# A transformer block on one Trainium2 core: retention on dense query columns, slot tables by one product, final scaling four tiles behind

## What is computed

```python
proj = h @ w_in                      # 4688 columns, two parallel head groups
y_a = dsa_attention(qa, ka, va, qi, ki, wi)    # indexer scores, top-256 keys, 8 heads
y_b = retention(qb, kb, vb, gb)                # 8 heads of 64
x = x + gt1 * (concat(y_a, y_b) @ w_o)
x = x + gt2 * hier_moe(h2)           # 2 of 32 SwiGLU experts for each token
return rmsnorm(x, g_final)
# retention, for each head, by chunks with a running state:
scores = (q @ k.T) * decay;  inner = scores @ v
cross  = (q @ state) * xi;   state = state * g_chunk + (k * zeta).T @ v
y = group_norm(inner + cross) * silu(g)
```

## Time and profile before

| | us |
|---|---|
| median of 3 runs | 1657.19 (1653.68 to 1657.38) |
| the profiled execution | 1657.88 |
| its span, first to last instruction | 1655.4 |
| PE busy | 1476.1 (89%) |
| DVE busy | 1124.7 (68%) |
| ACT busy | 913.5 (55%) |
| POOL busy | 267.4 (16%) |

### The profile page before, as it was taken

How to read it: one execution, slowest core, us unless ns; L and a number is a source line. 1 busy time by engine, 2 the same in 40 slices (tenths; PEclk the granted TensorE clock), 3 DMA queues, 4 the chain that set the end, 5 groups by cost and what they waited for, 6 DMA issues and landing times.

```text
span 1655.4 us, 21644 instructions
## 1 busy us (share of the span) xinstructions
PE 1476.1 (89%) x7444; PEld 1155.5 (70%) x7444; DVE 1124.7 (68%) x1511; ACT 913.5 (55%) x1231; POOL 267.4 (16%) x192
## 2 busy tenths in 40 slices
PE   3899999999999898888899967999999999999950
PEld 2587455888887787455666646888888888888840
DVE  6632798662256983434444365999999999999937
ACT  5321577879994111424444414777777777777722
POOL 0000110330001011200000001322322332332114
PEclk9899999999999999589999976999999999999985
DMA  9198543222324234211221017999999999999966
GB/s 369 61 340 317 207 153 115 96 108 97 121 71 134 71 121 148 91 51 65 80 66 45 22 51 273 378 402 401 403 400 400 393 401 398 397 394 398 362 239 256
DMA packets 102566, 368.01 MB, mean 222 GB/s; under 512 B 11232, under 2 KB 23648, under 8 KB 77792
## 3 DMA queue, kind: packets, MB, share of 16 engines
q1 hardware_dynamic: 74208, 291.58, 46.2%
q10 hardware_dynamic: 17024, 41.95, 6.6%
q0 software_dynamic: 11264, 33.57, 5.6%
HBM read 306.24 MB, written 69.21 MB: 227 GB/s over the span
## 4 chain that ended last, share of the span: by engine, by line
PE 76%; DVE 13%; ACT 4%; issue 3%; DMA 2%; POOL 2%; SPq 0%; DVEq 0%; ACTq 0%; POOLq 0%
PE PS L1638 19%; PE PS L1640 19%; PE PS L1639 19%; PE PS L1739 3%; PE PS L1762 2%; PE PS L1960 2%; PE PS L1848 2%; PE PS L1835 1%; DMA WK<-in_w_ada 1%; DVE wlo L1553 1%; DVE WK L1045 1%; PE PS L1695 1%; POOL BIG L730 1%; PE PS L1935 1%; DVE ACC L1158 1%
## 5 line engine op out<-in xcount | busy, mean ns | idle before, releaser
L1553 DVE TENSOR_TENSOR wlo<-raw,whi 128x2048 fp32r<-128x2048 f32 x192 | 435.8, 2285 | 36.4 <-ACT whi L956 34.9
L956 ACT ACTIVATE whi<-raw 128x2048 fp32r<-128x2048 f32 x192 | 364.0, 1913 | 130.1 <-DVE WK L1572 80.8
L1638 PE MATMUL PS<-whi,xhi 128*128 128x512 f32 x512 | 203.7, 398 | 7.3 <-DVE xlo L1559 6.1
L1640 PE MATMUL PS<-whi,xlo 128*128 128x512 f32 x512 | 201.1, 393 | 0.0
L1639 PE MATMUL PS<-wlo,xhi 128*128 128x512 f32 x512 | 200.1, 391 | 0.0
L837 ACT ACTIVATE KV<-ACC,WK 128x1024 int8<-128x1024 f32 (+4 forms) x160 | 147.5, 926 | 23.7 <-DVE WK L1181 21.1
L1638 PE MATMUL PS<-KVR,BIGR 128*128 128x512 f32 x320 | 127.0, 397 | 1.1 <-ACT WK L822 1.1
L694 POOL COPY wcol<-tw 128x1 f32 (+1 forms) x32 | 64.3, 2009 | 381.7 <-DVE WK L1590 377.3
L1640 PE MATMUL PS<-KVR,BIGR 128*128 128x512 f32 x320 | 124.9, 390 | 0.0
L1639 PE MATMUL PS<-KVR,BIGR 128*128 128x512 f32 x320 | 124.5, 389 | 0.0
L1638 PEld LDWEIGHTS PS<-whi,xhi 128*128 128x128 f32 x512 | 97.0, 190 | 27.6 <-DVE xlo L1559 7.0
(11 more groups left out here) (331 smaller groups left out, 2960.4 us busy)
## 6 DMA issues: line engine op xcount, KB each, us to landing
raw<-in_w_gate SPq DMA_DIRECT2D x64, 1024.0 KB, 7.3
raw<-in_w_up SPq DMA_DIRECT2D x64, 1024.0 KB, 7.8
raw<-in_w_down SPq DMA_DIRECT2D x64, 1024.0 KB, 7.2
y_dram<-zero ACTq DMA_DIRECT2D x8, 3072.0 KB, 11.3
WK<-in_w_ada POOLq DMA_DIRECT2D x16, 1024.0 KB, 7.5
y_dram<-WK ACTq DMA_DIRECT2D x32, 512.0 KB, 7.0
KV<-in_w_in SPq DMA_DIRECT2D x5, 2048.0 KB, 10.0
KV<-in_x SPq DMA_DIRECT2D x16, 512.0 KB, 5.2
```

The source lines that it names most:

```text
L956: nc.scalar.activation(whi[:, slot], raw[:, q], ACT.Copy).then_inc(G("m_hi"), 1)
L1553: V.tensor_tensor(wlo[:, slot], raw[:, q], whi[:, slot].bitcast(F32), ALU.subtract)\
L1638: mm(out_, x_hi, w_hi, start=first, stop=False)
L1640: return mm(out_, x_lo, w_hi, start=False, stop=final)
```

## The change

Four things, told by what they do.

Retention. The turned queries are kept dense (`qT`, 512 columns) and not block-diagonal. Scores are eight products of 64 rows and 128 columns, one for a head, the even heads on rows 0 to 63 and the odd ones on rows 64 to 127, in different banks. The constant `carry` that scales the state after each tile is zero outside the two diagonal blocks, so that one product of 128 columns gives the state's part for two heads. ACT makes one copy of 128 rows instead of two of 64. POOL's memset of `qBD` goes.

Slot tables. `tbl` and `tw` come from one product of 100 columns for each group of copies, where there were two of 50. DVE therefore multiplies by the weights (`sw`) before it signals each half. `items` without the number of rounds is written first of all, SP reads the number of rounds only after the three written-out slots, and DVE splits the first gate half of slot 0 before it copies the tables.

Final stage. DVE scales tile t - 4 after it has added tile t, with cells of its own for each tile's sum, mean and root.

```diff
-    parts["carry"] = np.tile(np.repeat(np.exp(P * lg), HD)[None], (P, 1))
+    parts["carry"] = np.where(p[:, None] // HD == np.arange(HB * HD)[None] // HD % 2,
+                              np.repeat(np.exp(P * lg), HD)[None], 0.0)
...
+            rounds = rounds()
             with engine.Fori(0, rounds) as j:
...
-            rounds = nc.sync.value_load(items[0:1, 63:64], min_val=1, max_val=MOST_ROUNDS)
...
+            def load_rounds():
+                sp.wait_ge(G("r_items"), 2)
+                return nc.sync.value_load(items[0:1, 63:64], min_val=1, max_val=MOST_ROUNDS)
...
-            for j in range(4):
-                pool.wait_ge(G(f"st_ev{j}"), 16 * 8)
-            own(nc.gpsimd.memset(WB["qBD"].rearrange("p j h n -> p (j h n)"), 0.0), G("b_clear"))
...
-                    act.wait_ge(G("b_clear"), 1)
-                pq = PS[:, 4, :].rearrange("p (j n) -> p j n", j=4)
-                own.go(A(WB["qBD"][0:64, :, 0, :], pq[0:64], ACT.Copy))
-                own.go(A(WB["qBD"][64:128, :, 1, :], pq[64:128], ACT.Copy), G("b_qbd"))
+                    for j in range(4):
+                        act.wait_ge(G(f"st_ev{j}"), 16 * 8)
+                own.go(A(WB["qT"], PS[:, 4, :].rearrange("p (j n) -> p j n", j=4), ACT.Copy), G("b_qbd"))
...
-                    own.go(V.tensor_tensor(WB["S"][:, 4 * half:4 * half + 4],
+                    own.go(V.tensor_tensor(WB["S"].rearrange("p (j a) n -> p a j n", a=2)[:, half],
...
+            dve.wait_ge(G("r_pe"), 3)
+            own(V.tensor_copy(items[0:1, 0:MAX_ITEMS], PS[0:1, 3, 0:MAX_ITEMS]), G("r_items"))
             for e, name in enumerate(("e1", "e2")):
                 own(V.tensor_tensor(WR["tmp"], WR[name], WR["V"], ALU.mult))
...
-                                       r16[:, some].unsqueeze(2).to_broadcast([P, 8, P]), ALU.is_equal), G("r_oh"))
-            own.wait()
-            for e in range(2):
-                some = slice(8 * e, 8 * e + 8)
+                                       r16[:, some].unsqueeze(2).to_broadcast([P, 8, P]), ALU.is_equal))
+                own.wait()
                 own.go(V.tensor_tensor(ohi[:, some, 1], ohi[:, some, 1],
                                        sw[:, e, :].unsqueeze(2).to_broadcast([P, T, TBL]), ALU.mult), G("r_oh"))
...
+            low(0, 0, GATE[0])
             dve.wait_ge(G("r_acc"), 1)
             own(V.tensor_scalar(tbl[:, :], PS[:, 2, 0:TBL], float(NO_TOKEN), None, ALU.add), G("r_done"))
-            dve.wait_ge(G("r_acc"), 2)
-            own(V.tensor_copy(tw[:, :], PS[:, 4, 0:TBL]), G("r_done"))
+            own(V.tensor_copy(tw[:, :], PS[:, 2, TBL:2 * TBL]), G("r_done"))
...
-                if t >= 2:
-                    f_finish(t - 2)
+                if t >= LAG:
+                    f_finish(t - LAG)
...
-                for j in range(4):
-                    last = mm(PS[:, 6 + j // 2, 256 * (j % 2):256 * (j % 2) + 256], WB["kT"][:, j, :],
-                              WB["qBD"][:, j].rearrange("p h n -> p (h n)"), start=True, stop=True)
+                for h in range(HB):
+                    rows = slice(HD * (h % 2), HD * (h % 2) + HD)
+                    last = mm(PS[:, 6 + h % 2, P * (h // 2):P * (h // 2) + P], WB["kT"][rows, h // 2, :],
+                              WB["qT"][rows, h // 2, :], start=True, stop=True)
...
-                    o = PS[:, 4, HD * h:HD * h + HD]
-                    if t >= 1:
-                        mm(o, WB["qBD"][:, h // 2, h % 2, :], WB["st"][:, h // 2, HD * (h % 2):HD * (h % 2) + HD],
+                    if t >= 1 and h % 2 == 0:
+                        mm(PS[:, 4, HD * h:HD * h + 2 * HD], WB["qT"][:, h // 2, :], WB["st"][:, h // 2, :],
                            start=True, stop=False)
-                    last = mm(o, WB["S"][:, h, :], WB["v"][:, HD * h:HD * h + HD], start=(t == 0), stop=True)
+                    last = mm(PS[:, 4, HD * h:HD * h + HD], WB["S"][:, h, :], WB["v"][:, HD * h:HD * h + HD],
+                              start=(t == 0), stop=(t == 0 or h % 2 == 1))
...
-            for a, bank in ((0, 2), (1, 4)):
-                for n in range(2 * T):
-                    if n % T == 0:
-                        pe.wait_ge(G("r_oh"), 2 * a + n // T + 1)
-                    last = mm(PS[:, bank, 0:TBL], WR["ohp"][:, n], WR["ohi"][:, n, a], start=(n == 0), stop=(n == 2 * T - 1))
-                last.then_inc(G("r_acc"), 1)
+            for n in range(2 * T):
+                if n % T == 0:
+                    pe.wait_ge(G("r_oh"), n // T + 1)
+                last = mm(PS[:, 2, 0:2 * TBL], WR["ohp"][:, n], WR["ohi"][:, n].rearrange("p a n -> p (a n)"),
+                          start=(n == 0), stop=(n == 2 * T - 1))
+            last.then_inc(G("r_acc"), 1)
```

More of the change, by code:

```diff
@@ L38 @@
 SPLIT_AT = 4
+LAG = 4
 STEP_SPEND = 5.0
@@ L300, in block_kernel @@
         items = sb("items", [1, 64], I32)
-        f_ms = [small[:, 55 + s:56 + s] for s in range(2)]
-        f_rs = [small[:, 57 + s:58 + s] for s in range(2)]
+        f_sq, f_ms, f_rs = [[small[:, T * n + t:T * n + t + 1] for t in range(T)] for n in range(3)]
         PS = ctx.enter_context(nc.psum_tensor("PS", [P, 8, 512], F32))
@@ L452, in steps @@
             step(2 * rounds + PEELED, 1, True)
+            return rounds
         def count(rounds):
@@ L725, in f_root @@
                 pool.wait_ge(G("norm_ms"), 2 * T + t + 2)
-                own(tt(f_rs[t % 2], f_ms[t % 2], expo[:, 0:1], ALU.pow), G("norm_rs"))
+                own(tt(f_rs[t], f_ms[t], expo[:, 0:1], ALU.pow), G("norm_rs"))
             for t in range(T):
@@ L1006, in _ @@
                 act.wait_ge(G("f_sum"), t + 1)
-                own(A(WF["sq"], WF["x"][t], ACT.Square, accum_out=small[:, 53 + t % 2:54 + t % 2]), G("norm_sq"))
+                own(A(WF["sq"], WF["x"][t], ACT.Square, accum_out=f_sq[t]), G("norm_sq"))
         @block.vector
@@ L1480, in _, with low @@
                     own(V.tensor_copy(L[:, TILES[i], :], PS[:, 7, 0:36]), G("b7_free"))
+            def low(i, s, q):
+                n, slot = place(i, s, q)
+                dve.wait_ge(G("m_hi"), n + 1)
+                V.tensor_tensor(wlo[:, slot], raw[:, q], whi[:, slot].bitcast(F32), ALU.subtract)\
+                    .then_inc(G("m_lo"), 1)
             spend(1000.0, last_choice)
@@ L1505, in _ @@
                 own(V.tensor_reduce(WR["row"][:, e], WR["tmp"], X_AXIS, ALU.add))
-            own(V.tensor_scalar(WR["h"][0:1, 0:MAX_ITEMS // 2], c("even")[0:1, :], end[0:1, NE - 1:NE], None,
-                                ALU.is_lt))
-            own(V.tensor_reduce(WR["h"][0:1, 32:33], WR["h"][0:1, 0:MAX_ITEMS // 2], X_AXIS, ALU.add))
-            own(V.tensor_scalar(WR["h"][0:1, 32:33], WR["h"][0:1, 32:33], (PEELED + 1) / 2, None, ALU.subtract))
-            own(V.tensor_copy(items[0:1, 63:64], WR["h"][0:1, 32:33]))
-            dve.wait_ge(G("r_pe"), 3)
-            own(V.tensor_copy(items[0:1, 0:MAX_ITEMS], PS[0:1, 3, 0:MAX_ITEMS]), G("r_items"))
             row16 = WR["row"].rearrange("p e t -> p (e t)")
@@ L1595, in _ @@
             dve.wait_ge(G("m_w"), 1)
-            for q in GATE:
-                low(0, 0, q)
+            low(0, 0, GATE[1])
             low_rows(0, 0)
-            steps(dve, rounds, step)
+            steps(dve, lambda: rounds, step)
             low_hidden(count(rounds) - 1)
@@ L1608, in f_finish @@
                 dve.wait_ge(G("norm_rs"), 2 * T + t + 2)
[L1609 removed]
+                own(V.scalar_tensor_tensor(xf, xf, f_rs[t], WF["gf"], ALU.mult, ALU.mult), G("f_out"))
             def f_mean(t):
[L1613 removed]
                 dve.wait_ge(G("norm_sq"), 2 * T + t + 1)
[L1615 removed]
+                own(V.tensor_scalar(f_ms[t], f_sq[t], 1.0 / D, EPS, ALU.mult, ALU.add), G("norm_ms"))
             for t in range(T):
@@ L1624, in _ @@
                     f_mean(t - 1)
-                if t >= 2:
-                    f_finish(t - 2)
+                if t >= LAG:
+                    f_finish(t - LAG)
             f_mean(T - 1)
-            f_finish(T - 2)
-            f_finish(T - 1)
+            for t in range(T - LAG, T):
+                f_finish(t)
         @block.tensor
```

24 lines of the change are left out of this document (10 added, 14 removed).

## The result

| | before | after |
|---|---|---|
| median of 6 runs, us | 1656.57 (1653.68 to 1657.38) | 1642.53 (1640.74 to 1645.89) |
| the profiled execution | 1657.88 | 1644.57 |
| its span | 1655.4 | 1642.6 |
| mean granted clock of PE | 0.940 | 0.941 |

What follows compares the result with a forecast made beforehand. Bounds: retention's chain of waits over PE, ACT and DVE; the experts' first product start; DVE in the final stage. Gains 7.9 + 3.9 + 5.3 = 17.1 from 1657.88 gave 1640.8, forecast 1640 us, range 1634 to 1647.5.

Steps and rivals of the forecast that it cites:

- so 0.7 saved for a tile: Retention, scores of a tile: sixteen records on alternating row halves take 1.0 us instead of 1.73, saving 0.7.
- The factor from the earlier trace: Retention scores: 0.57, from attention's products on two halves (1.99 us against 3.46), with half-row passages inside; 0.57 x 1.73 = 1.0 us.
- times 0.43 that is -1.2: Retention, scores of tile 2: 2.91 us at a clock just recovering, cut by 1.2 us.
- the cap at the mask of tile 5: Retention from 574.6 us: PE would get 2 us ahead, but tile 5's values need the mask ending at 603.32: only -0.4.
- Rival 1: Retention: row halves bring nothing, loads or columns going one after another; total gain 13.8, 1643.5 us; chance 0.12.
- rival 4: More than forecast: the clock rises in the table products and DVE's limit at 603.32 yields; 1635 us; chance 0.07.
- rival 2: Slot tables: gather queues behind weights asked for earlier, lands after 9.1 us, experts start 1.2 later than before; 1645 us; chance 0.08.
- one is done ahead of the tables: Slot tables: one of DVE's two low halves precedes the tables, the other runs under the gather; PE starts at 1013.2, -3.9 us.
- under 1 us: Final stage, sign to look for: DVE's wait ahead of the first scaling, 6.30 us before, is cut to under 1 us.
- Rival 3: Final stage: the fourth and fifth pairs land too late to fill the wait; it brings 1.5; 1644 us; chance 0.06.
- DVE's cover: Retention, tiles 3 and 4 (523.5 to 574.6 us): DVE is the chain, so nothing gained; without DVE worth 3 us.
- Rival 5: Retention: alternating halves empty the array at each change, +3.8 us for a tile, so slower; 1674 us; chance 0.02.

Runs made afterwards that it cites:

- the repetition: The changed kernel run again, unchanged, as the base of the runs beside it: 1644.92 us (ratio 0.993).
- the order of the heads: The changed kernel with the heads' scores in the order 0, 2, 4, 6, 1, 3, 5, 7, so halves alternate only once: 1647.45 us (ratio 0.9942).
- The runs with and without relief: Planner's STEP_SPEND 3.5 (relief) instead of 5.0: 1631.98 us in the changed kernel (ratio 0.9859), 1649.83 in the kernel before (0.9972).

## Why the prediction was right, and where its sizes were off

**Retention: 7.9 forecast, 6.45 in the profile.** The shape was right. Counted from the first score of each execution, the kernel after wins 1.6 us up to the scores of tile 2 (forecast 0.7 and 0.6), 1.1 from there to the end of the tile's values (2.1), nothing from there to the mask of tile 5 (nothing), and 3.75 from that mask to the end (4.5). Two terms were mis-sized. The first is "so 0.7 saved for a tile". The factor from the earlier trace rows was to contain the passages into and out of the half-row form, but these add 0.1 us to each of four steps here, the last ones in the product behind. Saved were 0.53 at tile 0, counted without the step ahead of it, 0.45 at tile 6 and 0.46 at tile 7: 0.7 us less over the three tiles that the forecast counts beside tile 2. The second is "times 0.43 that is -1.2" for the scores of tile 2. Up to the start of its values only 0.2 came out, 1.0 less. What counts there is when the clock is low, not the length of the records; the repetition, at full clock there, wins 1.8 at this place and 7.5 in all. Two smaller errors point opposite ways: the cap at the mask of tile 5 and the values behind it brought 1.1 us instead of 1.3, and the way from tile 0 to tile 2 brought 1.1 instead of 0.6, for which I have no cause. How near the term of tile 2 comes is in part luck: one execution wins 1.0 us less there than forecast and another 0.6 more.

**Rival 1**, that halves bring nothing, is refuted by the order of the heads. Its mechanism is real within one half: there a record follows every 0.11 us, and sixteen of them take 1.64, near the estimated 1.7 that the prediction worked out from the Trainium skill, "TensorE: Matmul & The Clock Gate", section "LDWEIGHTS (loading the stationary operand)". Alternating, they take 1.09, which that rule alone does not give.

**The slot tables: 3.9 forecast, 3.9 in the profile, 3.6 alone by the ratio.** The sum is right by luck: two errors cancel. The table products took 5.96 us and not 6.95, since their clock rose, as rival 4 allowed; the gather landed 1.1 later than forecast, a small form of rival 2. That "one is done ahead of the tables" mattered was wrong: the half can go back without loss. What pays is the one product where there were two. I also did not ask what the early half sets free: a buffer, and with it a transfer in the gather's way.

**The final stage: 5.3 forecast, 5.5 in the profile, 4.6 alone by the ratio.** The mechanism was as told. The wait left was 1.34 us, where "under 1 us" had been named. Rival 3 did not come about: the fourth and the fifth pair were both added ahead of the first scaling, and only one addition waited, 0.45 us. The 5.5 is one pair of profiles. Over all of them it is 41.3 to 42.8 us from the first addition to the end in four with the old lag and 35.7 to 38.1 in seven with four tiles, by the means 4.9 less.

**DVE's cover** was put at 3 us for tiles 3 and 4. The runs with and without relief give 3.6 (10.0 less 6.45), or 2.5 against the repetition (7.5).

**The sum.** In the profiles: 6.45 of retention, 3.9 of the tables and 5.55 of the final stage are 15.9, less the 3.3 by which retention's first score record is late: 12.6, where the spans differ by 12.8. Without the late start the forecast of 17.1 would have been 1.2 too much. The medians say 14.0, and 10.9 in the repetition, so stages of one pair of profiles promise more than the medians hold. A part of it can be the start of retention, which came 0.8 us later on the mean with the new retention; for the rest I have no cause.

**Rival 5**, the slower one, needed 0.43 us for a head. A head costs 1.09 / 8 = 0.14. The Trainium skill, "TensorEngine Tiling (Array Packing)", section "Key Properties", puts the drain on a change of mode and not of tile; the runs agree, with 0.91 and 0.92 us for the product behind one change of half and behind seven, and with pairs that follow each other every 0.11 us.

## What to carry to other kernels

Before a cut on one engine is counted, ask piece by piece which engine is the chain, and then whether the order of the covering engine's work can be changed: here one constant of a planner was worth as much in the changed kernel (12.9 us) as the whole rewrite (10.9 to 14.0), though only 6.0 in the kernel before, and the rewrite's part in retention brought 2.5 to 3.6 us more with it. Products on half of the rows paid here only where the halves alternate. Work moved early may free a buffer and so send a transfer ahead of the one that everything waits for; if nothing waits for the moved work, leave it where it was.

## What was not expected of the hardware

- Sixteen records of 64 rows and 128 columns, weights loaded for each, take 1.09 us when the halves alternate (a pair every 0.111 us) and 1.64 when they change once (a record every 0.111 us on one half). The way into and the way out of the half-row form cost some 0.2 us each once a tile, whether the halves changed once or seven times.
- Waits of PE cost more than their length: with most of those in 550 to 604 us gone, the granted clock there went from 0.90 to 1.00, PE was idle for 5.3 us less in retention, and retention was 8.5 us shorter.
- A low stretch of the clock behind 2.3 us of idle PE fell into the scores of tile 2 in one execution, behind them in another, and was absent in a third.
- The same instructions in 166 to 210 us ran at a granted clock between 0.88 and 1.00 in different executions, which moves everything behind them by up to 3.6 us.
- With one weight transfer sent 1.2 to 1.4 us ahead of the gather, its landing came 0.4 to 1.8 us later than in the three profiles without it (4.3 to 4.4 us).
